# Layer one's q, k and z turned by VectorE and DMAs instead of TensorE, and PLE's last chunk moved to the end

## The chip, the cores and the metric

One core of a Trainium2 chip runs the kernel. The metric is the device time of one execution in microseconds, the median of three runs. TensorE (PE) multiplies and transposes through PSUM, VectorE (DVE) and ScalarE (ACT) do the elementwise work, GpSimd (POOL) and SyncE (SP) issue the DMAs.

## What is computed

A decoder trunk of two layers over 256 tokens, model width 2048, 16 heads of 128. Layer one (the change's layer) is stick-breaking attention without positions; layer two is softmax attention over shared rotary keys and values. Each layer has a gate path and a second step with PLE ("per-layer embedding", `p @ w_ple`):

```python
q, k, v, z = jnp.split(x @ w_in, 4, axis=-1)
o = stick_breaking_attention(split_heads(q), split_heads(k), split_heads(v))
y = (merge_heads(o) * jax.nn.silu(z)) @ w_out
x = layer_norm(DEEPNORM_ALPHA * x + y, ln_g[i], ln_b[i])
x = x + (p[i] @ w_ple[i]) * jax.nn.sigmoid(x @ w_ple_gate[i])
```

Everything is float32. The kernel keeps that accuracy by splitting each operand in a high part (float32r) and the rest, and by three products: high by high, high by low, low by high.

## The kernel before

**Pieces.** All weight matrices are read in pieces of 256 rows by 512 columns (512 KB), 388 in all. A piece goes through one pipeline: SP loads it to one of four `raw` buffers, ACT writes its high part to one of eight `w_hi` buffers (L417), DVE the rest to `w_lo` (L676), and PE runs 12 matmuls of 512 columns on it (L1077 to L1079: two k tiles, two token tiles, three products). ACT may split piece n + 8 as soon as PE has used piece n; so PE has seven to eight pieces in hand, and ACT and DVE do one split after each piece of PE, plus the steps that the code puts behind it. Eight pieces make a chunk: all 2048 rows against 512 columns, summed in one half of PSUM's `acc`.

**Order.** Each engine's program is written out by hand, by the index of a piece in its chunk (`after={4: [...]}` is the step behind the fifth piece), and engines meet only in semaphores. Layer one goes in four groups of four heads; a group's chunks are q, k, v, z. Attention of group g lies between the pieces of its v and z chunks and the next group's q chunk. An engine does its program in order: a step that waits holds everything behind it on that engine.

**Turning.** The projections come out with tokens on partitions, while the scores need the head's features there, and so does the gated product. In before, DVE copies q, k and z from `acc` to SBUF (`evacuate`, L696, at the chunk's end, behind its eighth split). PE then transposes them with eight 128x128 transposes each to PSUM's `aux`: q behind the fifth piece of the k chunk (`q_turn`), k behind the third piece of the v chunk (`k_turn`, both L1104), z behind the third piece of the next q chunk (`z_turn`, L1170). ACT and DVE make the parts of q and k from `aux` (`q_copies` L440 and L441, `queries_lo`, `k_copies` L446 and L447, `keys_lo` L729), and ACT takes SiLU of z from there. PE needs q's and k's parts for `key_scores`, behind the fifth and the sixth piece of the v chunk (L1121).

**POOL** has little in layer one: one load of p and two tables early, then, once the last group's values are weighed, the residual (`load_res`, L361).

**Second step.** Behind the output projection, PE has four pieces of PLE (one for each 512 columns), and between them it turns the normalised x (`ln_turn`), which DVE scales (`full_quarter` L870) and ACT and DVE split (L430, L691) for the gate matrix. The gate's chunks follow. At the end of layer two ACT takes the sigmoid of the last gate chunk in two halves of tokens (L630), DVE multiplies with PLE (L943) and adds the residual (L946), and SP stores.

Of the kernel before, what the change touches and what calls it, by code (L numbers as in the profile page):

```python
# [29 lines left out]
P = 128  # L30
# [6 lines left out]
WARM_UPS = 14  # L37


def build(nc, xt, x, pt, w_in_a, w_out_a, w_kv, w_in_b, w_out_b, w_ple, w_ple_gate,  # L40
# [25 lines left out]
    N_GATE[1] = N_PLE[1] + G  # L66
    PIECES = N_GATE[1] + G * PC
# [22 lines left out]
    with ExitStack() as ctx:  # L90
# [3 lines left out]
        def sem(name):  # L94
# [59 lines left out]
        qn, kn, vn_a, zn_a = (big0[:, i * TT * COLS:(i + 1) * TT * COLS].rearrange(tokens, t=TT)  # L154
                              for i in range(4))
# [11 lines left out]
        offset = heads[:, D:2 * D]  # L167
        rope_tmp = heads[:, 0:HT].rearrange("p (t h d) -> p t h d", t=TT, d=DH)
# [8 lines left out]
        p_act = act0[:, :, KT - PIECE_K:KT, :]  # L177
        aux_b = aux[:, :].rearrange("p (b n) -> p b n", n=COLS)
# [85 lines left out]
        x2_ready = sem("dve_x2_ready")  # L264
        piece_used = sem("pe_piece_used")
        tile_0_done = sem("pe_tile_0_done")
        qT_psum = sem("pe_qT_psum")
# [13 lines left out]
        def _(sp):  # L281
# [50 lines left out]
            load_out_ple_gate(1, w_out_b[0])  # L332
            with sp.Fori(0, G - 1) as c:
# [3 lines left out]
            for t in range(TT):  # L337
                sp.wait_ge(x2_ready, 2 * G + t)
                sp.dma_start(out[t * P:(t + 1) * P, (G - 1) * COLS:], columns(res[1], G - 1)[:, t]) \
                    .then_inc(out_stored, 16)  # L340
            sp.wait_ge(out_stored, 16 * (G - 1 + TT))
# [3 lines left out]
        def _(pool):  # L345
# [38 lines left out]
            pool.dma_start(ln_col[:, :, :, :], ln_cols).then_inc(tables_landed, 16)  # L384
            pool.wait_ge(pv_done, 2 * G)
# [25 lines left out]
        def _(act):  # L411
# [20 lines left out]
            def copy_qT(k, dst):  # L432

                act.wait_ge(qT_psum, k + 1)
                nc.scalar.activation(dst, aux_kt[0], ACT.Copy, scale=SCALE).then_inc(qT_ready, 1)

            def q_copies(k):

                act.wait_ge(qT_psum, k + 1)
                nc.scalar.activation(qT[:, :, P:T], aux_kt[0][:, :, P:T], ACT.Copy, scale=SCALE).then_inc(qT_ready, 1)  # L440
                nc.scalar.activation(q_parts[:, 0], aux_kt[0], ACT.Copy, scale=SCALE).then_inc(q_hi, 1)  # L441
# [16 lines left out]
            def k_copies_b(k):  # L458

                act.wait_ge(kT_psum, k + 1)  # L460
                nc.scalar.activation(kT[:, :, 0:P], aux_kt[1][:, :, 0:P], ACT.Copy).then_inc(kT_ready, 1)
                nc.scalar.activation(k1_parts[:, 0], aux_kt[1], ACT.Copy).then_inc(k_hi, 1)
# [31 lines left out]
            def silu_z(k, dst, src):  # L494
                act.wait_ge(zT_psum, k + 1)
                nc.scalar.activation(dst, src, ACT.Silu).then_inc(sz_ready, 1)
# [110 lines left out]

            def out_ple_gate(layer, after_out):
# [8 lines left out]
                pieces(n, n, count=G, before={  # L617
                    0: ple_step[0:1] + [lambda r=r: normalise(2 * layer, r, r) for r in x1]
                    + ple_step[1:2] + full_step[0:1] + ple_step[2:3] + full_step[1:2] + ple_step[3:4],
                    2: full_step[2:3]})  # L620
# [5 lines left out]
                if layer:  # L626
                    for t in range(TT):
                        act.wait_ge(*((tile_0_done, LAYERS + 1) if t == 0 else (piece_used, PIECES)))
# [43 lines left out]
        def _(dve):  # L672
# [24 lines left out]

            def softplus(k, b):
# [22 lines left out]
            def queries_lo(k):  # L721
                dve.wait_ge(q_hi, k + 1)
                nc.vector.scalar_tensor_tensor(out=q_parts[:, 1], in0=aux_kt[0], scalar=SCALE,
                                               in1=q_parts[:, 0].bitcast(F32), op0=ALU.mult, op1=ALU.subtract) \
                    .then_inc(q_lo, 1)

            def keys_lo(k):
                dve.wait_ge(k_hi, k + 1)
                nc.vector.tensor_tensor(k_parts[:, 1], aux_kt[1][:, :, 0:P], k_parts[:, 0].bitcast(F32),  # L729
                                        ALU.subtract).then_inc(k_lo, 1)  # L730
# [47 lines left out]

            def k_steps(k, n):
                return {4: [lambda: queries_lo(k)]} | chunk_end(n, 1, kn)  # L780
# [10 lines left out]
            def z_steps(k, n):  # L791
                return {0: [lambda: softplus_lo(k, 1)], 2: [lambda: mask_stick(k, 0)], 3: [lambda: mask_stick(k, 1)],
                        4: [lambda: stick_weights_lo(k, 0)], 5: [lambda: stick_weights_lo(k, 1)]} \
                    | chunk_end(n, 1, zn_a)

            def gate_steps(k):
                return {2: [lambda: gate_group(k, k, gt)], 3: [lambda: gated_lo(k, k, k + S_OUT[0])]}

            dve.wait_ge(consts_done, 12)
            pieces(0, 0, chunk_end(0, 0, qn))  # L800
            pieces(PC, 0, k_steps(0, PC))
            with dve.Fori(0, G - 1) as g:
# [3 lines left out]
                pieces(n + 2 * PC, 0, gate_steps(g) | chunk_end(n + 2 * PC, 0, qn))  # L806
# [86 lines left out]
            def add_ple(layer, c):  # L893
# [4 lines left out]
                dve.wait_ge(ple_evac, G * (layer + 1))  # L898
# [14 lines left out]
            def out_ple_gate(layer, after_out):  # L913
# [13 lines left out]
                pieces(N_PLE[layer], N_PLE[layer], count=G,  # L927
                       before={0: turned[1], 2: turned[2]})
# [6 lines left out]
                if layer:  # L935
                    c = G - 1
                    gain_and_offset(layer, c)
                    dve.wait_ge(ple_evac, 2 * G)
                    dve.wait_ge(x1_ready, 2 * G)
                    for t in range(TT):  # L940
                        r, gate = columns(res[1], c)[:, t], stage_tn[:, t]
                        dve.wait_ge(sig_ready, 2 * G + t)
                        nc.vector.tensor_tensor(gate, gate, columns(ple[1], c)[:, t], ALU.mult) \  # L943
                            .then_inc(chunk_evac, 1)
                        dve.wait_ge(chunk_evac, C_GATE[1] + G + t)
# [115 lines left out]
        def _(pe):  # L1061
# [46 lines left out]
            def q_turn(k, c):  # L1108
                pe.wait_ge(chunk_evac, c + 1)
                if not isinstance(k, int) or k > 0:  # L1110
                    pe.wait_ge(gated, k)
                transposes(qn, aux_kt[0], qT_psum)

            def k_turn(k, c):
                pe.wait_ge(chunk_evac, c + 1)
                transposes(kn, aux_kt[1], kT_psum)

# [7 lines left out]
            def key_scores(k, b):  # L1125

                pe.wait_ge(qT_ready, k + 1)
# [3 lines left out]
                for h in (2 * b, 2 * b + 1):  # L1131
                    s = aux_b[:, h]
                    three_passes(s[:, 0:T], lambda i, h=h: k_parts[:, i, h], lambda i, h=h: q_parts[:, i, h], True)
                    mm = nc.tensor.matmul(s[:, T:SC], kT[:, h, P:T], qT[:, h, P:T], start=False, stop=True,
# [28 lines left out]
            def z_turn(k, c):  # L1163

                pe.wait_ge(chunk_evac, c + 1)
                for i in range(HG):
                    for t in range(TT):
                        bank = aux_b[:, 2 * (i // 2) + 1]
                        at = (i % 2) * T + t * P
                        mm = nc.tensor.transpose(bank[:, at:at + P], zn_a[:, t, i * P:(i + 1) * P], ident[:, :])  # L1170
                mm.then_inc(zT_psum, 1)

            def after_k(k, c):
                return {4: [lambda: q_turn(k, c - 1)]}

            def after_v(k, c):
                return {2: [lambda: k_turn(k, c - 1)], 4: [lambda: key_scores(k, 0)],
# [7 lines left out]
            def z_step(k, c):  # L1185
                return {2: [lambda: z_turn(k, c)]}

# [7 lines left out]
            chunk(PC, 0, act0, 1, 1, after=after_k(0, 1))  # L1195
            pe.wait_ge(masks_done, 1)
            with pe.Fori(0, G - 1) as g:
# [4 lines left out]
                chunk(n + 2 * PC, 0, act0, 0, c + 2, after=z_step(g, c + 1))  # L1202
                chunk(n + 3 * PC, 0, act0, 1, c + 3, after=after_k(g + 1, c + 3))
# [21 lines left out]
            def ple_and_gate(layer):  # L1225
# [11 lines left out]
                for c in range(G):  # L1237
# [11 lines left out]
                pe.wait_ge(ple_evac, layer * G + G)  # L1249
# [3 lines left out]
                if layer:  # L1253
                    c = G - 1
                    chunk(c * PC + n, n, act0, c % 2, c + c0, last=True)

# [5 lines left out]
            out_projection(0, z_step(G - 1, C_OUT[0] - 1))  # L1262
# [113 lines left out]
```

## Time and profile before

| | us |
|---|---|
| median of 3 runs | 1171.24 (1170.37 to 1171.37) |
| the profiled execution's own time | 1170.72 |
| its span, first to last instruction | 1168.8 |
| PE busy | 1161.9 (99%) |
| DVE busy | 740.9 (63%) |
| ACT busy | 591.1 (51%) |
| POOL busy | 21.3 (2%) |

The profile covers one execution. PE's busy time counts from each matmul's start to its modelled end, and matmuls overlap, so what a matmul costs is read from the distance between two starts. The granted TensorE clock is full over the span. The trace's timeline lists instructions with start and duration, and in brackets how long the engine had been idle and who released it.

### The profile page before, as it was taken

How to read it: one execution, taken by the hardware profiler on the slowest of the kernel's cores; microseconds unless marked ns; L12 is line 12 of the kernel's file. 1: busy time of each engine (PE TensorE's matmuls, PEld its weight loads, DVE VectorE, ACT ScalarE, POOL GpSimd, SP SyncE). 2: the span in 40 equal slices, each digit the busy share in tenths (PEclk: the TensorE clock that was granted, in tenths of full speed). 3: DMA queues.
4: the chain of work that ended last, by engine and by line, in shares of the span. 5: the costliest groups of instructions: out<-in, count | busy, mean ns of one | idle time of the engine just before them, and what ended most of it. 6: DMA issues, size and time to landing. Idle time of an engine off the chain costs nothing.

```text
span 1168.8 us, 15615 instructions
## 1 busy us (share of the span) xinstructions
PE 1161.9 (99%) x5484; PEld 971.4 (83%) x5484; DVE 740.9 (63%) x786; ACT 591.1 (51%) x669; POOL 21.3 (2%) x43
## 2 busy tenths in 40 slices
PE   9999999999999999999999999999999999999998
PEld 7888888888888888888888888888888888888886
DVE  6765556556556556688777665446677666656863
ACT  6665465456446543455444445544555545435541
POOL 1000000000000000000000000000000000000000
PEclk9999999999999999999999999999999999999999
DMA  9855656665565776457765655655545575763671
GB/s 307 287 161 178 181 162 178 179 181 161 165 194 156 241 253 200 137 184 237 232 198 162 197 180 182 193 181 164 169 155 178 167 244 175 252 195 112 211 252 41
DMA packets 112618, 221.49 MB, mean 189 GB/s; under 512 B 6929, under 2 KB 8977, under 8 KB 112065
## 3 DMA queue, kind: packets, MB, share of 16 engines
q1 hardware_dynamic: 110032, 209.74, 57.7%
q0 software_dynamic: 2544, 11.19, 2.7%
q8 instruction: 27, 0.44, 0.1%
q14 instruction: 15, 0.11, 0.0%
HBM read 216.71 MB, written 4.19 MB: 189 GB/s over the span
## 4 chain that ended last, share of the span: by engine, by line
PE 95%; DVE 2%; DMA 1%; ACT 1%; issue 0%; SPq 0%; ACTq 0%; DVEq 0%
PE acc L1077 29%; PE acc L1079 29%; PE acc L1078 29%; PE aux L1104 2%; PE aux L1121 2%; DVE w_lo L676 1%; PE aux L1145 1%; DVE stage L870 1%; PE aux L1159 1%; DMA raw<-in_w_ple_gate 1%; PE aux L1308 0%; DMA raw<-in_w_in_a 0%; DVE act L691 0%; PE aux L1079 0%; PE aux L1078 0%
## 5 line engine op out<-in xcount | busy, mean ns | idle before, releaser
L676 DVE TENSOR_TENSOR w_lo<-raw,w_hi 128x1024 fp32r<-128x1024 f32 x388 | 471.7, 1224 | 358.5 <-ACT w_hi L417 357.2
L417 ACT ACTIVATE w_hi<-raw 128x1024 fp32r<-128x1024 f32 x388 | 409.7, 1060 | 471.3 <-PE acc L1079 424.5
L1077 PE MATMUL acc<-w_hi,act 128*128 128x512 f32 x1552 | 611.9, 394 | 0.2 <-DVE w_lo L767 0.2
L1079 PE MATMUL acc<-w_hi,act 128*128 128x512 f32 x1552 | 605.1, 390 | 0.0
L1078 PE MATMUL acc<-w_lo,act 128*128 128x512 f32 x1552 | 604.1, 389 | 0.0
L1079 PEld LDWEIGHTS acc<-w_hi,act 128*128 128x128 f32 x1552 | 291.3, 188 | 61.8
L1077 PEld LDWEIGHTS acc<-w_hi,act 128*128 128x128 f32 x1552 | 291.5, 188 | 58.6 <-issue 1.0
L1078 PEld LDWEIGHTS acc<-w_lo,act 128*128 128x128 f32 x1552 | 291.7, 188 | 58.1
L430 ACT ACTIVATE act<-stage 128x1024 fp32r<-128x1024 f32 (+1 forms) x12 | 12.7, 1061 | 33.8 <-DVE stage L870 33.8
L513 ACT ACTIVATE heads<-aux,neg_max 128x128 f32<-128x128 f32 (+1 forms) x32 | 13.0, 419 | 23.7 <-DVE neg_max L1000 23.7
L691 DVE TENSOR_TENSOR act<-stage,act 128x1024 fp32r<-128x1024 f32 (+1 forms) x12 | 14.7, 1226 | 14.3 <-ACT act L430 14.3
L870 DVE TENSOR_SCALAR stage<-aux,ln_col 128x256 f32<-128x256 f32 x48 | 22.8, 538 | 0.9 <-PE aux L1104 0.9
L1104 PEld LDWEIGHTS aux<-ident,big 128*128 128x128 f32 x128 | 14.9, 140 | 2.1
L1104 PE MATMUL aux<-ident,big 128*128 128x128 f32 x128 | 16.6, 272 | 0.0
L696 DVE TENSOR_SCALAR big<-acc 128x1024 f32<-128x1024 f32 x12 | 14.6, 1218 | 0.0
L701 DVE SCALAR_TENSOR_TENSOR heads<-aux,heads 128x768 f32<-128x768 f32 x8 | 7.6, 954 | 10.8 <-ACT heads L483 10.8
L430 ACT ACTIVATE act<-heads 128x1024 f32 (+1 forms) x8 | 8.5, 1062 | 10.4 <-DVE heads L752 10.0
L691 DVE TENSOR_TENSOR act<-heads,act 128x1024 f32 (+1 forms) x8 | 9.8, 1225 | 5.7 <-ACT act L430 5.2
L417 ACT ACT_TABLE_LOAD x9 | 11.5, 1283 | 0.2
L630 ACT ACTIVATE stage<-acc 128x512 f32<-128x512 f32 x2 | 1.2, 598 | 19.1 <-PE acc L1079 19.1
L891 DVE TENSOR_TENSOR big<-big,heads (+1 forms) x8 | 9.8, 1225 | 0.9
L943 DVE TENSOR_TENSOR stage<-stage,big 128x512 f32<-128x512 f32 x2 | 1.4, 688 | 14.0 <-ACT stage L630 14.0
(148 smaller groups left out, 617.5 us busy)
## 6 DMA issues: line engine op xcount, KB each, us to landing
raw<-in_w_in_a SPq DMA_DIRECT2D x124, 512.0 KB, 3.7
raw<-in_w_ple_gate SPq DMA_DIRECT2D x64, 512.0 KB, 4.8
raw<-in_w_in_b SPq DMA_DIRECT2D x64, 512.0 KB, 3.7
raw<-in_w_kv SPq DMA_DIRECT2D x64, 512.0 KB, 3.7
raw<-in_w_out_a SPq DMA_DIRECT2D x32, 512.0 KB, 4.4
raw<-in_w_out_b SPq DMA_DIRECT2D x32, 512.0 KB, 4.9
heads<-in_ln_rows POOLq DMA_DIRECT2D x4, 1024.0 KB, 8.2
raw<-in_w_ple SPq DMA_DIRECT2D x8, 512.0 KB, 4.6
```

Source lines behind the costliest of these rows:

```text
L417: nc.scalar.activation(w_hi[:, r], raw[:, r % RAWS], ACT.Copy).then_inc(hi_ready, 1)
L430: nc.scalar.activation(quarter(dst[:, 0], c), src, ACT.Copy).then_inc(act_hi, 1)
L513: last = nc.scalar.activation(prob[:, b, h, lo:hi], aux_b[:, 2 * b + h, lo:hi], ACT.Exp, bias=neg_max[:, b, i:i + 1], accum_out=row_sum[:, ...
L676: nc.vector.tensor_tensor(w_lo[:, r], raw[:, r % RAWS], w_hi[:, r].bitcast(F32), ALU.subtract) \
L691: nc.vector.tensor_tensor(quarter(dst[:, 1], c), src, quarter(dst[:, 0], c).bitcast(F32), ALU.subtract).then_inc(act_ready, 1)
L696: nc.vector.tensor_scalar(dst, acc_of(parity), 1.0, None, ALU.mult).then_inc(chunk_evac, 1)
L870: last = nc.vector.tensor_scalar(stage_kt[:, i], aux_kt[pair][:, i], g, b, ALU.mult, ALU.add)
L1077: nc.tensor.matmul(dst, hi, w_hi[:, r, i], start=begin, stop=False)
L1078: nc.tensor.matmul(dst, hi, w_lo[:, r, i], start=False, stop=False)
L1079: mm = nc.tensor.matmul(dst, lo, w_hi[:, r, i], start=False, stop=end)
L1104: mm = nc.tensor.transpose(dst[:, i, t * P:(t + 1) * P], src[:, t, i * P:(i + 1) * P], ident[:, :])
L1121: mm = nc.tensor.matmul(dst, lhs(a), rhs(b), start=start and i == 0, stop=True, skip_group_check=True)
```

## The change

Layer one's q, k and z are no longer transposed by PE. At the end of their chunks DVE writes them to SBUF as independent 32x32 transposes (`turn_squares`), four by four squares for each 128x128 block, laid out so that what belongs to one group of 32 partitions is contiguous. POOL then issues 16 DMAs of 32 partitions by 256 elements (1 KB a partition) for each of the three (`exchange`), which bring each square to its partition group. ACT and DVE make the parts from the buffers that the DMAs write (`kT_x`, `qT_x`, `gt_x`, in `heads`), with access patterns in steps of 32. `aux` isn't used for q, k and z of layer one any more.

In layer two the fourth PLE piece is issued last, behind the gate's last chunk, in three parts (first token tile, then the second in two halves of 256 columns), from a copy of p's parts (`keep_p`), and DVE reads these parts from PSUM.

```diff
+            def exchange(turned, count, dst, src, moved):
+                pool.wait_ge(turned, count)
+                for a in range(NS):
+                    for g in range(NS):
+                        pool.dma_start(dst[g * SQUARE:(g + 1) * SQUARE, a * HT // NS:(a + 1) * HT // NS],
+                                       src[a * SQUARE:(a + 1) * SQUARE, g * HT // NS:(g + 1) * HT // NS]) \
+                            .then_inc(moved, 16)
+            for g in range(G):
+                exchange(chunk_evac, g * 4 + 1, heads[:, HT:2 * HT], qn, q_moved)
+                exchange(chunk_evac, g * 4 + 2, heads[:, 0:HT], kn, k_moved)
+                exchange(chunk_evac, g * 4 + 4, heads[:, 2 * HT + 4 * SC:], zn, z_moved)
             pool.wait_ge(pv_done, 2 * G)
             load_res(0, x)
...
             def k_copies(k):
-                act.wait_ge(kT_psum, k + 1)
-                nc.scalar.activation(kT[:, :, P:T], aux_kt[1][:, :, P:T], ACT.Copy).then_inc(kT_ready, 1)
-                nc.scalar.activation(k_parts[:, 0], aux_kt[1][:, :, 0:P], ACT.Copy).then_inc(k_hi, 1)
+                act.wait_ge(k_moved, k * MOVED + MOVED)
+                nc.scalar.activation(by_square(k_own), kT_x[:, 1::TT], ACT.Copy).then_inc(kT_ready, 1)
+                nc.scalar.activation(by_square(k_parts[:, 0]), kT_x[:, 0::TT], ACT.Copy).then_inc(k_hi, 1)
...
             def silu_z_group(k):
                 act.wait_ge(act_ready, k + S_OUT[0])
-                silu_z(k, gt, aux[:, :].rearrange("p (b s n) -> p b s n", b=2, s=2)[:, :, 1])
+                act.wait_ge(z_moved, k * MOVED + MOVED)
+                nc.scalar.activation(by_square(sz_a), gt_x, ACT.Silu).then_inc(sz_ready, 1)
...
+            def turn_squares(n_end, parity, dst):
+                dve.wait_ge(piece_used, n_end)
+                nc.vector.transpose(dst.rearrange("q (p h t c) -> q t h p c", p=NS, h=HG, t=TT),
+                                    acc_of(parity).rearrange("q t (h p c) -> q t h p c", p=NS, h=HG)) \
+                    .then_inc(chunk_evac, 1)
...
             def after_v(k, c):
-                return {2: [lambda: k_turn(k, c - 1)], 4: [lambda: key_scores(k, 0)],
+                return {4: [lambda: key_scores(k, 0)],
                         5: [lambda: key_scores(k, 1)]}
...
                 pe.wait_ge(p_ready, layer + 1)
-                for c in range(G):
+                for c in range(G - layer):
...
+                if layer:
+                    turn(2)
...
                     chunk(c * PC + n, n, act0, c % 2, c + c0, last=True)
+                    last_ple_product()
```

On ACT, in layer one's v chunk, the waits of the copies of k (`heads<-aux` and `k_parts<-aux`) stand like this before:

```order
56 L417 ACTIVATE w_hi<-raw 128x1024 [waits pe_piece_used]
57 L445 REGISTER_ALU
58 L446 ACTIVATE heads<-aux 128x4x128 [waits pe_kT_psum]
59 L447 ACTIVATE k_parts<-aux 128x512
60 L414 ISA
61 L416 REGISTER_ALU [waits dma_w_landed3]
```

and after:

```order
56 L457 ACTIVATE w_hi<-raw 128x1024 [waits pe_piece_used]
57 L485 ISA
58 L486 ACTIVATE big<-heads 128x512 [waits dma_k_moved]
59 L487 ACTIVATE k_parts<-heads 128x512
60 L454 ISA
61 L456 REGISTER_ALU [waits dma_w_landed3]
```

Their place is the same; they wait for the 16 DMAs now and not for PE's transposes.

On POOL, before, from the early tables to layer norm's rows:

```order
19 L383 DMA cos_sin<-in_rope 128x256
20 L384 DMA ln_col<-in_ln_cols 128x96
21 L361 DMA big<-in_x 128x2x512 [waits pe_pv_done]
22 L361 DMA big<-in_x 128x2x512 x3
23 L370 DMA heads<-in_ln_rows 128x2048 [waits dve_operand_ready]
```

and after, where the pattern of two rows comes twelve times ahead of `in_x`:

```order
19 L409 DMA cos_sin<-in_rope 128x256
20 L410 DMA ln_col<-in_ln_cols 128x96
21 L417 DMA heads<-big 32x256 [waits dve_chunk_evac]
22 L417 DMA heads<-big 32x256 x15
23 L417 DMA heads<-big 32x256 [waits dve_chunk_evac]
24 L417 DMA heads<-big 32x256 x15
```

POOL gets 192 DMAs, and the residual's load stands behind the last of them.

On DVE, at the very end, before (the product with PLE and the sum, for two token tiles):

```order
514 L891 TENSOR_TENSOR big<-big,heads 128x2x512 [waits dve_gained]
515 L943 TENSOR_TENSOR stage<-stage,big 128x512 [waits act_sig_ready,dve_x1_ready,act_ple_evac]
516 L946 TENSOR_TENSOR big<-big,stage 128x512 [waits dve_chunk_evac]
517 L943 TENSOR_TENSOR stage<-stage,big 128x512 [waits act_sig_ready]
518 L946 TENSOR_TENSOR big<-big,stage 128x512 [waits dve_chunk_evac]
```

and after:

```order
516 L1002 TENSOR_TENSOR stage<-aux,stage 128x512 [waits pe_last_ple,act_sig_ready,dve_x1_ready]
517 L1004 TENSOR_TENSOR big<-big,stage 128x512 [waits dve_last_product]
518 L1002 TENSOR_TENSOR stage<-aux,stage 128x256 [waits pe_last_ple,act_sig_ready]
519 L1004 TENSOR_TENSOR big<-big,stage 128x256 [waits dve_last_product]
520 L1002 TENSOR_TENSOR stage<-aux,stage 128x256 [waits pe_last_ple,act_sig_ready]
521 L1004 TENSOR_TENSOR big<-big,stage 128x256 [waits dve_last_product]
```

DVE's last products wait for PE's PLE parts, three of them instead of two.

## Rows read from the trace of the kernel before

**Rows 1.** The page: busy times, and the chain that ended last by engine

```profile
PE 1161.9 (99%) x5484; PEld 971.4 (83%) x5484; DVE 740.9 (63%) x786; ACT 591.1 (51%) x669; POOL 21.3 (2%) x43
...
PE 95%; DVE 2%; DMA 1%; ACT 1%; issue 0%; SPq 0%; ACTq 0%; DVEq 0%
```

**Rows 2.** ACT's timeline around `q_turn`: start, duration, instruction, idle before

```profile
136.80 1.06 ACT L417 ACTIVATE w_hi<-raw 128x1024 fp32r<-128x1024 f32 x1 [1.66 <-PE acc L1079]
139.53 1.06 ACT L417 ACTIVATE w_hi<-raw 128x1024 fp32r<-128x1024 f32 x1 [1.67 <-PE acc L1079]
...
143.17 1.06 ACT L417 ACTIVATE w_hi<-raw 128x1024 fp32r<-128x1024 f32 x1 [1.18 <-PE acc L1079]
145.89 1.06 ACT L417 ACTIVATE w_hi<-raw 128x1024 fp32r<-128x1024 f32 x1 [1.66 <-PE acc L1079]
```

**Rows 3.** The chain in order of time: q's, k's and z's turns of one group

```profile
139.43 0.87 PE aux L1104 x8
156.68 0.87 PE aux L1104 x8
...
208.33 0.87 PE aux L1170 x8
```

**Rows 4.** DVE's timeline at the end of the same group's k chunk

```profile
149.98 1.23 DVE L676 TENSOR_TENSOR w_lo<-raw,w_hi 128x1024 fp32r<-128x1024 f32 x1 [1.77 <-ACT w_hi L417]
151.12 1.22 DVE L696 TENSOR_SCALAR big<-acc 128x1024 f32<-128x1024 f32 x1
```

**Rows 5.** ACT's, DVE's and PE's timelines: from k's turn to its scores

```profile
157.68 0.58 ACT L446 ACTIVATE heads<-aux 128x512 f32<-128x512 f32 x1
158.15 0.59 ACT L447 ACTIVATE k_parts<-aux 128x512 fp32r<-128x512 f32 x1
...
158.95 0.69 DVE L729 TENSOR_TENSOR k_parts<-aux,k_parts 128x512 fp32r<-128x512 f32 x1
...
162.84 0.52 PE L1121 MATMUL aux<-q_parts,k_parts 128*128 128x256 f32 x3
```

**Rows 6.** POOL's timeline: its DMA issues

```profile
23.63 0.88 POOL L366 DMA_DIRECT2D stage<-in_pt  x1 [20.22 <-PE acc L1079]
24.51 0.58 POOL L383 DMA_DIRECT2D cos_sin<-in_rope  x1
25.08 0.54 POOL L384 DMA_DIRECT2D ln_col<-in_ln_cols  x1
394.43 2.88 POOL L361 DMA_DIRECT2D big<-in_x  x4 [368.81 <-PE aux L1159]
```

**Rows 7.** DMA issues: count, size of one, median us to landing; GB/s by slice

```profile
x_spill<-big POOLq DMA_DIRECT2D x4, 512.0 KB, 3.2
out<-big SPq DMA_DIRECT2D x2, 256.0 KB, 2.5
cos_sin<-in_rope POOLq DMA_DIRECT2D x1, 128.0 KB, 4.6
...
GB/s 307 287 161 178 181 162 178 179 181 161 165 194 156 241 253 200 137 184 237 232 198 162 197 180 182 193 181 164 169 155 178 167 244 175 252 195 112 211 252 41
```

**Rows 8.** DVE's timeline beside POOL's issues at 394 us

```profile
394.16 1.23 DVE L676 TENSOR_TENSOR w_lo<-raw,w_hi 128x1024 fp32r<-128x1024 f32 x1 [2.71 <-ACT w_hi L417]
```

**Rows 9.** PE, ACT and DVE timelines, layer two's PLE and gate start

```profile
1071.15 1.03 PE L1104 MATMUL aux<-ident,big 128*128 128x128 f32 x8
1075.56 0.47 PE L1077 MATMUL acc<-w_hi,act 128*128 128x512 f32 x1
...
1071.61 1.23 DVE L691 TENSOR_TENSOR act<-stage,act 128x1024 fp32r<-128x1024 f32 x1 [1.13 <-ACT act L430]
1090.51 1.23 DVE L691 TENSOR_TENSOR act<-stage,act 128x1024 fp32r<-128x1024 f32 x1 [1.13 <-ACT act L430]
```

**Rows 10.** All engines' timeline at the end

```profile
1163.39 0.39 PE L1079 MATMUL acc<-w_hi,act 128*128 128x512 f32 x1
...
1163.82 0.60 ACT L630 ACTIVATE stage<-acc 128x512 f32<-128x512 f32 x1 [0.76 <-PE acc L1079]
...
1165.24 0.69 DVE L946 TENSOR_TENSOR big<-big,stage 128x512 f32<-128x512 f32 x1
```

More of the change, by code:

```diff
@@ L153, in build @@
         tokens = "p (t n) -> p t n"
-        qn, kn, vn_a, zn_a = (big0[:, i * TT * COLS:(i + 1) * TT * COLS].rearrange(tokens, t=TT)
-                              for i in range(4))
+        qn, kn, vn_a, zn = (big0[:, i * TT * COLS:(i + 1) * TT * COLS] for i in range(4))
+        vn_a = vn_a.rearrange(tokens, t=TT)
+        q_scaled = qn.rearrange("p (h t) -> p h t", t=T)
+        k_own = kn[:, 0:HG * P].rearrange("p (h t) -> p h t", t=P)
         q_all = big0[:, :].rearrange("p (h t) -> p h t", t=T)
@@ L332, in _ @@
             load_out_ple_gate(1, w_out_b[0])
+            load(N_LAST, N_LAST % SPLITS, w_ple[1], 0, G - 1)
             with sp.Fori(0, G - 1) as c:
@@ L336, in _ @@
                              columns(res[1], c)).then_inc(out_stored, 16)
[L337 to L341, printed above, removed]
+            for i, (t, lo, hi) in enumerate(LAST_PARTS):
+                sp.wait_ge(x2_ready, 2 * G + i)
+                sp.dma_start(out[t * P:(t + 1) * P, (G - 1) * COLS + lo:(G - 1) * COLS + hi],
+                             columns(res[1], G - 1)[:, t, lo:hi]).then_inc(out_stored, 16)
+            sp.wait_ge(out_stored, 16 * (G - 1 + len(LAST_PARTS)))
         @block.gpsimd
@@ L606, in x2_hi, with keep_p @@
                 operand_hi(act1, aux_kt[0], c)
+            def keep_p():
+                act.wait_ge(p_ready, LAYERS)
+                act.wait_ge(piece_used, N_PLE[1])
+                nc.scalar.activation(p_last, p_act.bitcast(F32), ACT.Copy).then_inc(p_kept, 1)
             def out_ple_gate(layer, after_out):
@@ L615, in out_ple_gate @@
                                        [lambda c=c: full_hi(k + c, c) for c in range(G)])
[L617 to L620, printed above, removed]
+                turns = {0: ple_step[0:1] + [lambda r=r: normalise(2 * layer, r, r) for r in x1]
+                         + ple_step[1:2] + full_step[0:1] + ple_step[2:3] + full_step[1:2] + ple_step[3:G - layer]}
+                turns |= {1: full_step[2:3], 2: [keep_p]} if layer else {2: full_step[2:3]}
+                pieces(n, n, count=G - layer, before=turns)
                 n = N_GATE[layer]
@@ L626, in out_ple_gate @@
                 if layer:
+                    pieces(n + (G - 1) * PC, n, count=1)
                     for t in range(TT):
-                        act.wait_ge(*((tile_0_done, LAYERS + 1) if t == 0 else (piece_used, PIECES)))
+                        act.wait_ge(*((tile_0_done, LAYERS + 1) if t == 0 else (piece_used, N_LAST)))
                         act.wait_ge(x2_ready, 2 * G - 1)
@@ L926, in out_ple_gate @@
                           + [lambda r=r: normalise(r, r) for r in x1] + turned[0]})
-                pieces(N_PLE[layer], N_PLE[layer], count=G,
-                       before={0: turned[1], 2: turned[2]})
+                pieces(N_PLE[layer], N_PLE[layer], count=G - layer,
+                       before={0: turned[1], 2 - layer: turned[2]})
                 n = N_GATE[layer]
@@ L936, in out_ple_gate @@
                     c = G - 1
+                    pieces(n + c * PC, n, count=1)
                     gain_and_offset(layer, c)
-                    dve.wait_ge(ple_evac, 2 * G)
                     dve.wait_ge(x1_ready, 2 * G)
-                    for t in range(TT):
-                        r, gate = columns(res[1], c)[:, t], stage_tn[:, t]
+                    for i, (t, lo, hi) in enumerate(LAST_PARTS):
+                        r, gate = columns(res[1], c)[:, t, lo:hi], stage_tn[:, t, lo:hi]
                         dve.wait_ge(sig_ready, 2 * G + t)
-                        nc.vector.tensor_tensor(gate, gate, columns(ple[1], c)[:, t], ALU.mult) \
-                            .then_inc(chunk_evac, 1)
-                        dve.wait_ge(chunk_evac, C_GATE[1] + G + t)
+                        dve.wait_ge(last_ple, i + 1)
+                        nc.vector.tensor_tensor(gate, aux_b[:, i, lo:hi], gate, ALU.mult).then_inc(last_product, 1)
+                        dve.wait_ge(last_product, i + 1)
                         nc.vector.tensor_tensor(r, r, gate, ALU.add).then_inc(x2_ready, 1)
@@ L1106, in transposes @@
                 mm.then_inc(signal, 1)
[L1108 to L1116, printed above, removed]
             def three_passes(dst, lhs, rhs, start):
@@ L1125, in key_scores @@
             def key_scores(k, b):
+                if not isinstance(k, int) or k > 0:
+                    pe.wait_ge(gated, k)
                 pe.wait_ge(qT_ready, k + 1)
@@ L1194, in _ @@
             chunk(0, 0, act0, 0, 0, quarters=S_X)
-            chunk(PC, 0, act0, 1, 1, after=after_k(0, 1))
+            chunk(PC, 0, act0, 1, 1)
             pe.wait_ge(masks_done, 1)
@@ L1201, in _ @@
                 chunk(n + PC, 0, act0, 1, c + 1, after=after_z(g, c + 1))
-                chunk(n + 2 * PC, 0, act0, 0, c + 2, after=z_step(g, c + 1))
-                chunk(n + 3 * PC, 0, act0, 1, c + 3, after=after_k(g + 1, c + 3))
+                chunk(n + 2 * PC, 0, act0, 0, c + 2)
+                chunk(n + 3 * PC, 0, act0, 1, c + 3)
             c = C_OUT[0] - 2
@@ L1236, in ple_and_gate @@
                 pe.wait_ge(p_ready, layer + 1)
-                for c in range(G):
+                for c in range(G - layer):
                     n = N_PLE[layer] + c
@@ L1255, in ple_and_gate, with last_ple_product @@
                     chunk(c * PC + n, n, act0, c % 2, c + c0, last=True)
+                    last_ple_product()
+            def last_ple_product():
+                r = N_LAST % SPLITS
+                pe.wait_ge(lo_ready, N_LAST + 1)
+                pe.wait_ge(p_kept, 1)
+                for bank, (t, lo, hi) in enumerate(LAST_PARTS):
+                    for i in range(PIECE_K):
+                        p_hi_t, p_lo_t = (p_last[:, s, i, t * P:(t + 1) * P] for s in range(2))
+                        dst = aux_b[:, bank, lo:hi]
+                        nc.tensor.matmul(dst, p_hi_t, w_hi[:, r, i, lo:hi], start=i == 0, stop=False)
+                        nc.tensor.matmul(dst, p_hi_t, w_lo[:, r, i, lo:hi], start=False, stop=False)
+                        mm = nc.tensor.matmul(dst, p_lo_t, w_hi[:, r, i, lo:hi], start=False, stop=i == PIECE_K - 1)
+                    mm.then_inc(last_ple, 1)
             def x2_turn(c):
```

75 lines of the change are left out of this document (42 added, 33 removed).

## The prediction, on record before the changed kernel ran

> **What bounds the kernel now.** I read the page's busy times first, then the chain that ended last [rows 1]: PE is busy 99% of the span and makes 95% of the chain. So whatever leaves PE's program comes off the time one for one, as long as nothing that PE waits for becomes late. I then read the chain in order of time for the turns of one group [rows 3], ACT's timeline for what a turn really takes [rows 2], and the timelines of DVE, ACT and PE between the end of a k chunk and its scores [rows 4, 5], because that is the only place of layer one where a transposed operand is wanted soon. POOL's own rows [rows 6, 7] are the only ones that say anything of what the new path costs.
>
> **What is removed.** ACT's splits of weights start when PE has ended a piece, so their distance is a piece: 139.53 - 136.80 = 2.73 and 145.89 - 143.17 = 2.72 us without a turn, 143.17 - 139.53 = 3.64 us with one [rows 2]. A turn costs 0.92 us, a little over the 0.87 that the chain gives it [rows 3], since the matmul behind it starts late. There are three turns in each of four groups, 12 in all: 12 x 0.92 = 11.0 us off PE. All of it is on the path.
>
> **What takes its place, for k.** Before, k is in SBUF at 151.12 + 1.22 = 152.34 [rows 4], and PE turns it at 156.68 [rows 3] with time to spare. PE starts the scores at 162.84 [rows 5]; with k's turn gone PE is there 0.92 earlier, at 161.92. From the transposed k to the scores there are two copies on ACT and a subtraction on DVE: from 157.68 to 158.95 + 0.69 = 159.64, 1.96 us [rows 5]. The new forms have the same sizes, so I keep that. Handing over between engines costs about 0.1 us at either end. So the DMAs must have landed 161.92 - 1.96 - 0.1 = 159.86, and POOL starts at 152.34 + 0.1 = 152.44, if a 32x32 transpose of 1024 columns takes DVE as long as the copy that it replaces (1.22 us). 7.4 us are left for 16 issues and the last landing.
>
> An issue: the trace has no DMA of 32 partitions. Those of 128 rows take 0.58 and 0.54 us, those of 256 rows 0.72 (2.88 for four) and once 0.88 [rows 6]. They follow each other without a gap (24.51 - 23.63 = 0.88, 25.08 - 24.51 = 0.57), so these are distances too. From 128 to 256 rows adds 0.17; a straight line down to 32 rows gives 0.56 - 0.13 = 0.43. If the cost is flat below 128 rows it is 0.54. I take the middle, 0.48, since the nearest rows are those of 128 and part of their cost must depend on the rows; both ends are kept. 16 x 0.48 = 7.7 us (6.9 to 8.6).
>
> The landing: the spill of 512 KB lands 3.2 us after its issue [rows 7], 0.72 of it the issue itself. At the page's best rate, 307 GB/s [rows 7], 512 KB take 1.7 us; what is left is 0.8. A DMA of 32 KB adds 0.1, so 0.9 us from the end of the last issue to landing. The other end is the 2.5 us of a small store and the 4.6 of the table behind a full queue [rows 7].
>
> So k lands at 152.44 + 7.7 + 0.9 = 161.0, and PE waits 161.0 - 159.86 = 1.2 us in each group; with 0.43 for an issue 0.4, with 0.54 2.1. Four groups: **4.8 us lost** (1.6 to 8.4). Queued behind ACT's wait are its next weight splits, and DVE's behind ACT's. PE has seven to eight pieces of 2.72 us in hand, so ACT may be held for over 15 us before PE notices, and it needs only 1.06 us for each split when it catches up. The wait costs just what the scores wait.
>
> The Trainium skill, "DMA: Bandwidth & Descriptors", section on the anatomy of one DMA from GpSimd, gives some 2.0 us from a DMA's start to its end however small it is, where I have 0.48 + 0.9 = 1.4. By it each group would lose 0.6 us more and the sum would be 2.5 us higher; the spill's row is compatible with either.
>
> **q and z.** q's DMAs end some 10 us behind the q chunk's last split, and its copies stand behind the fifth piece of the next chunk, 13.6 us on: hidden. z's land later than PE's turn did; ACT's SiLU stands behind the third piece (8.2 us) and waits about 4 us. What hangs on it is the gated product, which PE needs only at the next group's scores, and in the last group at the thirteenth piece of the output projection, over 30 us on. Cover: the seven pieces in hand. Cost nothing. POOL's exchanges don't meet: chunks are 22 us apart and an exchange takes 8. The residual's load now stands behind the last z exchange, about 11 us later than before; its first part is wanted 14 pieces, 38 us, into the projection, so it is hidden too. The DMAs move 6 MB more over layer one's 390 us, 16 GB/s beside 160 to 180 [rows 7].
>
> **PLE's last chunk.** Layer two's fourth PLE piece, 12 matmuls, stood at a place where PE had work anyway. Without it the gate starts when quarter 0's low part is there, 1071.61 + 1.23 = 1072.84, and not at 1075.56 [rows 9]: 2.7 us earlier. But quarter 3's low part ends at 1090.51 + 1.23 = 1091.74 [rows 9], and the gate's seventh piece would now want it at about 1090.1. DVE has one split less ahead of it and ACT a copy more, so it comes at about 1090.5: 0.4 lost, 2.3 kept. At the end, PE does the same products behind the gate: 1.36 us for the first part, 0.7 for each half. Before, from PE's end (1163.39 + 0.23) to DVE's last (1165.24 + 0.69) it is 2.3 us [rows 10]. Now DVE starts its product 1.6 us after the gate's end, and needs 2 x 0.69 and 4 x 0.42 with small gaps: 4.7 us. 2.4 us lost, 0.2 back from a half-sized last store. Sum: 0 (from -0.7 to +1.5, if quarter 3 or the handing over is later).
>
> **Sum.** Against the profiled execution's 1170.7: -11.0 + 4.8 + 0 = 1164.5. The median of the runs is 0.5 above it, so 1165.0.
>
> **Rivals.**
> 1. *POOL is slower at issuing, and the change loses.* If a DMA's cost doesn't fall with its rows at all, 0.72 an issue: 16 x 0.72 = 11.5, PE waits 5.0 us a group, 20 in all, 1180. At 0.88 it is 7.6 a group, 1190. It loses from 0.62 us an issue on (where four waits reach 11.0 + 2). For it: the first of a row of issues took 0.88, and POOL never issued 16 in a row. Against it: the 0.54 and 0.58.
> 2. *DVE's transpose is slow.* At twice the copy's price, 1.22 more before POOL starts, the groups lose 4.9 us more: 1169.9, on the border of no change. DVE's rows in this trace run at one price for all 1024-column forms, but none of them transposes.
> 3. *POOL is locked out while DVE works.* Each of DVE's weight splits (1.23 of every 2.72 us) would hold POOL's descriptor writing up, so that an exchange of 7.7 us takes three splits, 3.7 us, more: 14.8 in all, 1180. Against it: POOL's four issues from 394.43 took 2.88, the usual 0.72 each, though a split ran from 394.16 to 395.39 [rows 6, 8]. The Trainium skill, "SBUF — State Buffer", section "SBUF: two separate sides", warns of exactly this for DVE operations that use both ports, and says that GpSimd then can't write descriptors. By that rule the sum would be 1180; the trace disagrees for this form of DVE instruction.
> 4. *Nothing waits.* Issues of 0.40 or less, or a landing faster than 0.9: 1160.
>
> **How the numbers follow.** The forecast's case (1161.5 to 1168.5) 0.50; nothing waits 0.11; slow issues 0.22, most of it slower; slow transposes 0.11, half of it no change and the rest to either side; lockout 0.06. A measurement tells about 0.2% (2.3 us) from no change: faster is below 1168.9, slower above 1173.6. Faster 0.50 + 0.11 + 0.03 = 0.64, no change 0.12, slower 0.24. The range goes from 1160, where nothing waits, to 1180, slow issues at 0.72, and leaves out the slowest issues and a little at the lower end.
>
> **What would show it.** In the trace of the changed kernel: pieces of layer one all 2.72 us apart but for the attention's own matmuls; POOL's 16 issues at 0.43 to 0.54 us; ACT's copy of k starting 8 to 9.5 us after the transpose; PE idle about 1.2 us ahead of the scores, four times, and nowhere else in layer one; the transposes at 1.2 us; DVE's last sum 4 to 5 us behind the gate's last matmul. It is wrong if an issue takes over 0.6 us, if the last landing comes over 2 us after the last issue, or if PE waits for weights in layer one.

## The result, and the profile after

The changed kernel takes 1190.51 us (median of 4 runs, 1189.59 to 1192.33) against 1171.07 of before: ratio 1.0169, 95% interval [1.0151, 1.0186]. It is slower by 19.4 us, where 6 us faster was forecast. The page of its profile, where it answers to [rows 1]: the PE share of the chain is down from 95% to 78%, and POOL, its DMAs and DVE have come in.

```profile
PE 1160.3 (98%) x5394; PEld 968.5 (81%) x5394; DVE 738.4 (62%) x788; ACT 590.7 (50%) x669; POOL 115.1 (10%) x235
...
PEclk9979999999998999999999999999999999999999
...
PE 78%; DMA 7%; DVE 5%; POOL 5%; issue 2%; ACT 2%; SPq 0%; ACTq 0%; DVEq 0%
...
L1169 PE MATMUL aux<-q_parts,k_parts 128*128 128x256 f32 x48 | 11.6, 364 | 22.5 <-DVE k_parts L784 22.5
...
L749 DVE STREAM_TRANSPOSE big<-acc 128x1024 f32<-128x1024 f32 x12 | 14.9, 1243 | 0.0
...
heads<-big POOLq DMA_DIRECT2D x192, 32.0 KB, 3.6
```

L1169 is the first matmul of the scores: PE now waits 22.5 us ahead of it, in four waits, one in each group. The slices of PEclk that read 7 and 8 are new: the granted clock falls there. The transposes take 1.24 us, like the copies that they replaced [rows 4]. A 32 KB DMA lands 3.6 us after its issue.

POOL's timeline has the issues of the second group's k, and the chain in order of time shows what follows them (start, duration, what):

```profile
161.72 7.81 POOL L417 DMA_DIRECT2D heads<-big  x16 [13.61 <-DVE big L749]
```

```profile
169.03 3.75 DMA heads<-big
...
173.34 0.62 ACT k_parts L487
173.98 0.70 DVE k_parts L784
...
174.82 0.59 PE aux L1169 x3
...
176.68 0.43 PE acc L1135
177.10 0.43 PE acc L1136
```

An issue takes 7.81 / 16 = 0.49 us. The last one ends at 161.72 + 7.81 = 169.53, and ACT can start at 172.80 only, 3.3 us later. PE's matmul ahead of the scores started at 171.07 and the scores start at 174.82: 3.75 us where 0.22 is usual. And the matmuls behind the wait stand 0.43 us apart instead of 0.23, half the clock.

The sum of the loss, from starts on PE's timeline. The waits ahead of the scores are 10.2, 3.5, 3.7 and 5.7 us, 23.1 in all (the page counts 22.5, from the modelled end of the matmul ahead). From the first scores to the second it is 3.94 us before (162.84 to 166.78), and now 6.57, 5.57, 5.58 and 5.98, so the low clock costs 2.6 + 1.6 + 1.6 + 2.0 = 7.9. Less 11.0 for the twelve turns gives +20.0, and the spans differ by 1189.4 - 1168.8 = 20.6.

### The profile page after: what moved, and what is told of

The parts are those of the page before. It is cut to its first block, busy times and chain, and to the rows that moved or that the text cites. A ratio compares the mean times of both kernels' runs of the same rounds, so it can differ in the third digit from the quotient of the medians.

```text
span 1189.4 us, 15631 instructions
## 1 busy us (share of the span) xinstructions
PE 1160.3 (98%) x5394; PEld 968.5 (81%) x5394; DVE 738.4 (62%) x788; ACT 590.7 (50%) x669; POOL 115.1 (10%) x235
## 4 chain that ended last, share of the span: by engine, by line
PE 78%; DMA 7%; DVE 5%; POOL 5%; issue 2%; ACT 2%; SPq 0%; ACTq 0%; DVEq 0%
PE acc L1135 24%; PE acc L1137 23%; PE acc L1136 23%; POOL heads L417 5%; DMA heads<-big 3%; DMA raw<-in_w_in_a 2%; DVE w_lo L724 2%; PE aux L1169 2%; PE aux L1162 2%; DMA raw<-in_w_out_a 1%; ACT w_hi L457 1%; DVE big L749 1%; PE aux L1195 1%; DVE stage L928 1%; DMA raw<-in_w_ple_gate 1%
## 5 line engine op out<-in xcount | busy, mean ns | idle before, releaser
L417 POOL DMA_DIRECT2D heads<-big x192 | 93.8, 497 | 306.4 <-DVE big L749 256.6
L1169 PE MATMUL aux<-q_parts,k_parts 128*128 128x256 f32 x48 | 11.6, 364 | 22.5 <-DVE k_parts L784 22.5
L438 POOL COPY heads<-big 128x512 f32 x4 | 3.0, 757 | 313.2 <-PE aux L1169 292.1
L1169 PEld LDWEIGHTS aux<-q_parts,k_parts 128*128 128x128 f32 x48 | 8.9, 241 | 24.4 <-issue 24.1
L807 DVE TENSOR_TENSOR heads<-aux,big 128x1024 f32<-128x1024 f32 x8 | 9.8, 1221 | 23.3 <-ACT big L545 23.3
L784 DVE TENSOR_TENSOR k_parts<-heads,k_parts 128x512 fp32r<-128x512 f32 x4 | 2.8, 693 | 26.8 <-ACT k_parts L487 26.8
L486 ACT ACTIVATE big<-heads 128x512 f32<-128x512 f32 x4 | 2.5, 629 | 27.1 <-DMA heads<-big 27.1
L749 DVE STREAM_TRANSPOSE big<-acc 128x1024 f32<-128x1024 f32 x12 | 14.9, 1243 | 0.0
```

Of the source, the lines that this page charges most:

```text
L417: pool.dma_start(dst[g * SQUARE:(g + 1) * SQUARE, a * HT // NS:(a + 1) * HT // NS], src[a * SQUARE:(a + 1) * SQUARE, g * HT // NS:(g + 1) ...
L749: nc.vector.transpose(dst.rearrange("q (p h t c) -> q t h p c", p=NS, h=HG, t=TT), acc_of(parity).rearrange("q t (h p c) -> q t h p c", p= ...
L1169: mm = nc.tensor.matmul(dst, lhs(a), rhs(b), start=start and i == 0, stop=True, skip_group_check=True)
```

## The experiments

Three questions are open. Is the loss all in layer one? What makes k late, the issues or the landing? And why is the first group's wait three times that of the second?

### PLE's last chunk alone

A switch for each of q, k and z chooses between the 32x32 squares with DMAs (True) and PE's turn as before (False):

```diff
+QX, KX, ZX = False, False, False
```

> Layer one's q, k and z are turned by PE as before; only PLE's last chunk stands last. The theory (the whole loss is in layer one's DMAs): no change that can be measured, 1171 us (from 1170.4 to 1172.6), no gap on PE in layer one, DVE's last sum 4 to 5 us behind the gate's last matmul and the gate started 2.3 to 2.7 us earlier. The rival (the PLE step carries part of the loss): 1175 or more.

1170.54 us, ratio 0.9996 [0.9987, 1.0006]. No change. On PE the gate's first matmul, and on DVE the last sums:

```profile
1073.48 0.47 PE L1170 MATMUL acc<-w_hi,act 128*128 128x512 f32 x1
```

```profile
1163.42 0.69 DVE L1037 TENSOR_TENSOR stage<-aux,stage 128x512 f32<-128x512 f32 x1 [14.92 <-PE aux L1367]
...
1165.99 0.43 DVE L1039 TENSOR_TENSOR big<-big,stage 128x256 f32<-128x256 f32 x1
```

The gate starts about 2.5 us earlier, once the 0.4 us are taken off by which this run stands later there (its weight split is at 1061.08, that of before at 1060.69), and the end is as much longer. The loss is in layer one.

### z alone by DMAs, and all but k

In the run z_only, and in k_by_pe:

```diff
+QX, KX, ZX = False, False, True
...
+QX, KX, ZX = True, False, True
```

> Only z goes by 32x32 transposes and DMAs; q and k are turned by PE; PLE's last chunk is last. The theory (z's path is hidden, each turn taken off PE gives its 0.92 us): 4 x 0.92 = 3.7 us under ple_only, about 1167.4, no gap on PE in layer one. The rival (64 more DMAs and ACT held for z make weights late): as ple_only or slower, with PE waiting for a weight part.

1166.12 us, ratio 0.9958 [0.9941, 0.9975], and no gap on PE in layer one. z's four turns come off at their price or a little more (4.4 us below ple_only, 3.7 forecast). ACT does wait for z's DMAs, 12 to 19 us over the four groups, and in this run it costs nothing: PE's pieces in hand cover it.

> q and z go by DMAs, k is turned by PE. The theory (three of the changed kernel's four waits are k's DMAs alone, but the first group's wait of 10.2 us has 7 us from q: q's DMAs land late, ACT and DVE are held and k leaves PSUM late): groups two to four without a gap, in the first group a gap of 2 to 3 us on PE ahead of k's turn, 1171 - 7.4 + 3 + 1 for the clock = 1167.5. The rival (the first group's wait is k's DMAs as well): no gap anywhere, 1163.8.

1166.19 us, ratio 0.9962 [0.9948, 0.9976]. One gap is left on PE, in the first group, ahead of k's turn:

```profile
58.62 0.39 PE L1172 MATMUL acc<-w_hi,act 128*128 128x512 f32 x1
61.69 0.99 PE L1197 MATMUL aux<-ident,big 128*128 128x128 f32 x7 [2.68 <-DVE big L768]
```

2.7 us, as the theory had it; the time is 1.3 us under its 1167.5, and the rival's 1163.8 and "no gap" do not hold. k's copy leaves PSUM late on DVE, though k itself has no DMA here. So the first group has a cause of its own.

### The first group: q's DMAs hold ACT, ACT holds DVE, DVE holds k

The chain of the changed kernel around the first group:

```profile
40.33 7.34 POOL heads L417 x15
47.67 5.53 DMA heads<-big
...
54.19 1.05 ACT q_parts L481
55.26 1.23 DVE q_parts L779
56.49 1.67 DVE w_lo L724 x2
...
58.68 1.22 DVE w_lo L724
59.90 1.17 DVE big L749
...
61.34 7.32 POOL heads L417 x15
68.66 3.68 DMA heads<-big
```

q's last DMA lands 5.5 us after its issue began, at 53.2. ACT had stood at its copy for 6.2 us, since 47.0, and the splits of ACT and DVE behind it are late when the chunk ends at about 50.5 (an estimate: PE was ready for the scores at 64.2, five pieces of 2.72 us later). k's transpose waits behind them in DVE's order and starts at 59.8 (59.81 on DVE's own timeline), 9.3 us behind the chunk's end and not 2.5 as in the second and third group.

The landing isn't all of it. The trace of before shows that this group has little time for q in any case:

```profile
38.94 1.22 DVE L696 TENSOR_SCALAR big<-acc 128x1024 f32<-128x1024 f32 x1
...
42.27 1.03 PE L1104 MATMUL aux<-ident,big 128*128 128x128 f32 x8
```

q is in SBUF 2.1 us before PE turns it; in the second group it is 10.1 us (the copy ends at 129.38, the turn is at 139.43 [rows 3]).

```diff
-                exchange(chunk_evac, g * 4 + 1, heads[:, HT:2 * HT], qn, q_moved)
+                if g > 0:
+                    exchange(chunk_evac, g * 4 + 1, heads[:, HT:2 * HT], qn, q_moved)
...
-            chunk(PC, 0, act0, 1, 1)
+            chunk(PC, 0, act0, 1, 1, after={4: [q_turn]})
```

> As the changed kernel, but the first group's q is turned by PE. The theory (ACT held for q in the first group makes k leave PSUM 7 us late): k's transpose in the first group starts 2.4 us behind its chunk's end as in the other groups, PE's wait falls from 10.2 to about 3.5 us, 1190.5 - 6.7 - 1.0 + 0.9 = 1183.7. The rival (the first group's DMAs are slow by themselves, in the start's traffic): wait of 9 us or more, 1190.

1183.64 us, ratio 1.0105 [1.0088, 1.0122]. The wait of the first group is now 3.8 us on PE's timeline, like the others (3.5, 4.0, 3.6); the line below is its first matmul of the scores. So the first group's cause is q. That the time meets the 1183.7 is luck in part: the first group still loses 2.7 us to the clock, where 1.0 less was expected, and the fourth group's wait fell by 2.2, which nobody expected.

```profile
69.63 0.98 PE L1175 MATMUL aux<-q_parts,k_parts 128*128 128x256 f32 x3 [3.65 <-DVE k_parts L790]
```

### Issues or bytes

```diff
-                exchange(chunk_evac, g * 4 + 2, heads[:, 0:HT], kn, k_moved)
+                pool.wait_ge(chunk_evac, g * 4 + 2)
+                for a in range(NS):
+                    pool.dma_start(heads[a * SQUARE:(a + 1) * SQUARE, 0:HT], kn[a * SQUARE:(a + 1) * SQUARE, :]) \
+                        .then_inc(k_moved, 16)
```

> As the changed kernel, but k's exchange is 4 DMAs of 32 partitions by 4 KB, which move the same 512 KB without the change of places (so the scores are wrong). The theory (the number of issues sets when k lands): k's issues take 2.0 us and not 7.8, PE's waits ahead of the scores fall by 5.8 us each, from 10.2, 3.5, 3.7, 5.7 to 4.4, 0, 0, 0, with most of the 7.9 us of low clock: 1165.5. The rival (the bytes behind the weight loads set it): the last landing comes 5 to 8 us after the last issue, and the time stays over 1180.

1172.75 us, ratio 1.002 [1.001, 1.003]. Between the two. The waits fell to 8.1, 0.5, 0 and 0.4 us, so the count of issues matters most. But the saving was not 5.8 us each: it was 2.1, 3.0, 3.7 and 5.3. In the second group:

```profile
159.06 1.94 POOL L425 DMA_DIRECT2D heads<-big  x4 [13.95 <-DVE big L752]
```

```profile
167.08 0.63 ACT L489 ACTIVATE big<-heads 128x512 f32<-128x512 f32 x1 [2.63 <-DMA heads<-big]
```

The issues end at 161.0 and ACT starts at 167.08: 6.1 us of landing, against 3.3 with 16 small DMAs. What was saved on POOL was half lost in the queue. Waits of 9.0 us, their clock (1.9) and the turns make about 1171. Of the 1.5 us that are left, the view of PE's waits has 1.4: two of 0.8 us, on `big` from DVE, come behind layer one's attention, where before has one of 0.2. Why this run has them wasn't followed up.

### The weight loads that go first

`hold` is given for the fifth piece of a z chunk only:

```diff
                 if not isinstance(n, int) or n >= RAWS:
                     sp.wait_ge(lo_ready, n - RAWS + 1)
+                if hold is not None:
+                    sp.wait_ge(k_moved, hold)
...
-                load_chunk(n + PC, 0, wa, g + 3 * G)
+                load_chunk(n + PC, 0, wa, g + 3 * G, g * MOVED + MOVED)
```

> As the changed kernel, but SP holds the load of the z chunk's fifth piece, and all loads behind it, until k's 16 DMAs have landed, in each group. The theory (k's last DMAs land 3.3 to 4.4 us behind the last issue because a 512 KB load of weights goes first): they land within 1.5 us of the last issue, PE's waits ahead of the scores fall by some 2.3 us each, with a little of the clock 1179. The rival (a DMA of this kind takes 3.5 us whatever else moves): waits unchanged, 1190, or slower where the held loads are missed.

1177.91 us, ratio 1.0053 [1.0036, 1.0069], 12.6 us under the changed kernel. The DMA view over k's exchange of the second group, first of the changed kernel, then of this one (GB/s in 40 slices of 0.4 us, and the issues):

```profile
GB/s 277 164 184 312 353 287 133 102 179 410 399 236 195 67 108 225 364 405 374 205 108 133 266 384 405 359 123 108 133 307 404 374 118 0 0 0 0 0 0 0
...
raw<-in_w_in_a SPq DMA_DIRECT2D x4, 512.0 KB, 4.1
heads<-big POOLq DMA_DIRECT2D x16, 32.0 KB, 3.2
```

```profile
GB/s 159 82 148 297 394 318 87 92 169 297 410 307 190 67 82 82 82 82 72 46 46 82 82 77 56 41 72 82 82 0 0 0 26 72 164 241 338 399 399 410
...
raw<-in_w_in_a SPq DMA_DIRECT2D x5, 512.0 KB, 4.6
heads<-big POOLq DMA_DIRECT2D x16, 32.0 KB, 1.7
```

With weight loads in between, the traffic comes in bursts of 400 GB/s, one for each load, and a small DMA lands 3.2 us after its issue. Once they are held, the traffic is 41 to 82 GB/s, 32 KB for each issue, and a small DMA lands after 1.7 us. The last issue ends at 158.98 + 7.82 = 166.80 and ACT starts at 168.00:

```profile
158.98 7.82 POOL L419 DMA_DIRECT2D heads<-big  x16 [13.95 <-DVE big L751]
```

```profile
168.00 0.63 ACT L488 ACTIVATE big<-heads 128x512 f32<-128x512 f32 x1 [3.62 <-DMA heads<-big]
```

1.2 us instead of 3.3. PE's waits fell by 1.9 to 2.2 us each, to 8.3, 1.5, 1.5 and 3.6, 8.4 in all; with them 3.1 us of low clock went.

The trace's records of single DMA transfers, which none of the views prints, show the order. In the changed kernel POOL issues a DMA every 0.49 us from 161.7 to 169.5, but the transfers of its queue start in four batches, from 163.2, 166.0, 168.8 and 170.8 us on, each at the end of a load's burst; from 164.4 to 166.0 only one starts. In this run, once the loads have stopped, 18 to 34 start in every slice of 0.4 us. The Trainium skill, "DMA: Bandwidth & Descriptors", section "Queues, rings and completion order", says that a DMA engine takes turns between the rows that have work, and that it drains a whole packet of one row, typically some 9 to 17 descriptors, before it switches. A load is 256 rows of 2 KB, 16 for each of the core's 16 DMA engines, so by that rule an estimate is that a small DMA can stand behind most of a load. The trace agrees: beside the loads it lands 1.5 us later, and 512 KB at 400 GB/s take 1.3 us.

### The clock behind a wait

```diff
+FILL = 15
...
+                if b == 0:
+                    for _ in range(FILL):
+                        nc.tensor.matmul(aux_b[:, 3], act0[:, 0, 0, 0:P], act0[:, 0, 0:2, :], start=True, stop=True,
+                                         skip_group_check=True)
                 pe.wait_ge(qT_ready, k + 1)
```

> As the changed kernel, with 15 matmuls of 512 columns (3.4 us) whose result nobody reads, ahead of PE's wait for the scores' operands. The theory (after each wait PE runs at 1.2 GHz for a while, which costs 2.6, 1.6, 1.6 and 2.0 us): in the second and third group PE is busy through the wait and the matmuls behind it keep their 0.23 us, the fourth keeps a part; 3 to 5 us less, 1186.5. The rival (the matmuls behind a wait are slow for another reason, such as their operands): 1190 to 1191, with distances of 0.43 us as before.

1184.17 us, ratio 1.0119 [1.0099, 1.014], 6.3 us under the changed kernel, by matmuls that compute nothing. The stretches of 20 us around the four waits, in the changed kernel and in this one (after the stretch and its length, busy us and count of PE, PEld, DVE, ACT and POOL; then the granted clock, the DMA share and GB/s):

```profile
60.00:80.00 20.00, 9.93 (x38) 8.17 (x37) 7.67 (x7) 7.27 (x9) 7.81 (x16) 0.66 0.68 221
160.00:180.00 20.00, 16.63 (x72) 13.64 (x71) 8.16 (x8) 8.19 (x10) 7.81 (x16) 0.91 0.64 189
```

```profile
60.00:80.00 20.00, 13.47 (x56) 11.13 (x55) 8.10 (x8) 7.70 (x9) 7.81 (x16) 0.83 0.67 216
160.00:180.00 20.00, 19.74 (x98) 16.42 (x96) 7.92 (x8) 8.89 (x11) 7.81 (x16) 1.00 0.62 187
```

In the second group PE is kept busy and the clock stays at 1.00, which is 2.4 GHz. The scores start at 174.86, as in the changed kernel (174.82), and the second scores follow after 4.01 us, not 5.57. The first group still idles for 6.7 us and still loses clock. So the slow matmuls behind a wait come from the idle engine, and not from their operands.

### The deadline moved, and both mended

```diff
-                return {4: [lambda: key_scores(k, 0)],
-                        5: [lambda: key_scores(k, 1)]}
+                return {5: [lambda: key_scores(k, 0)],
+                        6: [lambda: key_scores(k, 1)]}
```

ACT's and DVE's steps of the v chunk (k's copies, the exponentials, softplus) move by one piece with it, on top of q0_by_pe.

> As q0_by_pe, and the scores of layer one stand one piece later (behind the sixth and seventh piece of the v chunk), with the steps on ACT and DVE that go with them. The theory (the wait is a deadline missed by 3 to 6 us): each wait is one piece, 2.7 us, shorter: 0.8, 0.8, 1.0, 3.0 us, and the clock stays up in three of four groups: 1168. The rival (another step, the softplus chain ahead of the z chunk's third piece, takes the deadline's place): PE waits there instead and the time stays above 1175.

1165.04 us, ratio 0.9951 [0.9935, 0.9968]. Waits of 1.0, 1.2, 1.3 and 0.9 us; the fourth was expected at 3.0, from the changed kernel's 5.7, but q0_by_pe had already brought it to 3.6. One piece more of time, 2.7 us, took 18.6 us off: 10.6 of the waits, and 7.0 because the clock stays up as well.

With SP's hold of sp_holds on top, nothing should be left:

> later_q0 with SP's hold of the weight loads until k's DMAs have landed, as in sp_holds. The theory (what is left of the wait in later_q0, 0.9 to 1.3 us a group, is k's last landing behind a weight load): no gap on PE in layer one, 11 turns of 0.92 us off PE against ple_only's 1170.5: 1160.5. The rival (the held loads are missed, ACT or PE waits for weights behind the hold): 1163 or more, with PE waiting for a low part of a weight.

1160.41 us, ratio 0.991 [0.9894, 0.9925]: the fastest of all, 10.6 us under before. PE no longer waits for k. One wait that before doesn't have is left in its view of waits in layer one, on the softplus chain:

```profile
PE aux L1204 <- DVE sp_parts L807: 0.3, 1, 0.3
```

The simpler way, k in all groups and q in the first left to PE:

> k in every group, and q in the first, are turned by PE; the other q and z go by DMAs. The theory: no gap on PE in layer one, 7 turns of 0.92 us less than ple_only: 1164.1. The rival (the exchange has a cost of its own outside the scores' wait, which k_by_pe's 1166.2 hides): 1166 or more.

1163.74 us, ratio 0.9939 [0.9925, 0.9952], without a gap on PE in layer one. Both times are within 0.4 us of "ple_only less 0.92 for each turn", with 11 and 7 turns.

## Why the prediction was wrong

**The turns** were priced right. Where nothing waits, each one is worth about the 0.92 us read from [rows 2]: 1.1, 0.97 and 0.92 us against ple_only, for 4, 7 and 11 turns.

**The issues** were right: 0.49 us measured, 0.48 taken, from [rows 6]. **The transposes** were right: 1.24 us for 1.22. **PLE's chunk** was right at zero: DVE's last sum ends 4.7 us behind the gate's end, as worked out. **Rival 3**, POOL locked out by DVE, didn't happen: 16 issues take 7.8 us whatever DVE does, as [rows 8] had said.

**The landing was the first step that failed.** The forecast took 0.9 us from the last issue's end to landing, out of the spill's row [rows 7], and called 2.5 to 4.6 the other end. Measured: 3.3 us in the second group, 3.2 to 3.9 over the four; the prediction's own sign of being wrong, over 2 us, is met. The 0.9 describes the DMA without company, and sp_holds gives 1.2 for that. What was missed is that SP's queue puts a burst of 512 KB between one piece and the next, about every 2.7 us, and POOL's transfers start behind it. The bound at the other end was read but left out of the sum and of the range: landings of 3.2 to 3.9 instead of 0.9 cost 2.3 to 3.0 us in each group, 10.2 in all, and the upper ends of issue and landing were never added. A small term beside it: POOL starts 0.3 us behind DVE's transpose, not 0.1.

**"q: hidden" failed in the first group.** It was argued from the steady groups, where q is in SBUF early and ACT's pieces in hand cover the rest. In the first, before already leaves q only 2.1 us. By the forecast's own prices q lands at 40.16 + 0.1 + 7.7 + 0.9 = 48.9, when ACT has been ready for it since 47.0; at 53.2, where it landed, ACT has stood 6.2 us. This wait passes over DVE's in-order queue to k's transpose. The prediction looked for what PE misses when ACT waits, and not for what DVE has standing behind ACT. q0_by_pe puts it at 6.4 us of wait in the first group (10.2 against 3.8). The 6.9 us between the two times hold more than that: 2.2 us of wait from the fourth group as well, and 0.9 paid for the turn.

**The clock was no term of the sum.** In before PE never stood still in layer one once it had started, so no row priced it. The four waits cost 7.9 us on top of their 23.1. No rival had it either.

**The fourth group's wait** of 5.7 us is larger than the second's by 2.2, and the trace shows the first group's mechanism again:

```profile
353.98 1.06 ACT L480 ACTIVATE big<-heads 128x1024 f32<-128x1024 f32 x1 [4.12 <-DMA heads<-big]
...
360.57 1.24 DVE L749 STREAM_TRANSPOSE big<-acc 128x1024 f32<-128x1024 f32 x1
```

ACT stands 4.1 us for q, and k's transpose starts 3.9 us behind its chunk's end, not 2.5: 1.4 us. The last landing gives another 0.6 (3.9 against 3.3). What made q late comes from further back: z's exchange of the third group starts 2.6 us behind DVE's transpose (314.46 + 1.24 = 315.70), not 0.3, with nothing in the profile that it waits for:

```profile
318.35 7.82 POOL L417 DMA_DIRECT2D heads<-big  x16 [49.37 <-issue]
```

All seven runs with more than 128 of these DMAs have such a pause of 2.6 to 2.9 us, always ahead of the 129th; the runs with up to 128 have none. In q0_by_pe it falls ahead of q's exchange in the fourth group, and the wait there is 3.6. What the pause is stays open, and no run removed it alone.

Of the 25.5 us between forecast (1165.0) and time, the waits are 23.1 - 4.8 = 18.3 and the clock 7.9, which is 26.2; the rest is within what the runs scatter. Of the 18.3, the landings are 10.2, and q in the first and the fourth group 6.4 + 1.4.

Rival 1, that it loses, had the right sign and by chance nearly the right time, but by another mechanism.

## What to carry to other kernels

Work taken off the bounding engine pays only if the new path's last byte is there at the old deadline: work that path out to the end, with the DMA's landing measured beside the traffic that will run there, not alone, and add the upper ends of all its terms once. Follow an in-order wait through every queue that stands behind it, in the first round of a loop by itself, since little is in hand there. A path that misses by 1 to 4 us can be mended cheaply: move the consumer one piece later, and hold the bulk loads for the few microseconds in which the small DMAs fly.

## What the runs showed of the hardware

- A DMA of 32 partitions by 1 KB takes POOL 0.49 us to issue, one of 32 partitions by 4 KB as much (1.94 / 4); those of 128 rows took 0.54 to 0.58 [rows 6]. The count of DMAs is what costs.
- A DMA of 32 partitions by 1 KB, SBUF to SBUF, lands 1.7 us after its issue began where loads are held (sp_holds) and 3.2 to 3.6 (medians) beside loads of 512 KB, 5.5 at most, in the first group. Its transfers start in batches, at the ends of the loads' bursts.
- After waits of 3.5 to 10 us TensorE ran its next matmuls at half the clock (0.43 us for 512 columns, not 0.23), which cost 1.4 to 2.9 us each over all runs, 1.6 to 2.6 in the changed kernel. The longer wait didn't always cost more: 3.6 us cost 2.9 in sp_holds, 8.1 us cost 1.8 in k_four. After waits of 0.9 to 1.5 us (later_q0, sp_holds) it was under 0.1. Matmuls without a purpose in place of the wait kept the clock.
- DVE's 32x32 transposes of 1024 float32 columns from PSUM take 1.24 us, the price of a copy (1.22).
- POOL paused for 2.6 to 2.9 us ahead of the 129th of its small DMAs in all seven runs that issue more than 128. Why isn't known.
